# Pool branch of a hybrid decoder step as one stage: weights stationary, tokens moving

## The chip, the cores and the metric

One NeuronCore of a Trainium2 chip runs the whole program. The metric is the device time of one execution in microseconds.

## The reference

One layer for 1024 prompt tokens and 8 x 8 sample tokens, in float32. The part that matters here is the pool branch: the normed input times 512 columns of the input projection, causal means over 2, 4, 8 and 16 rows (one window for each group of 128 channels) minus the token itself, and a 128 x 128 mixing matrix per group.

```python
def pool_mix(ext, pos_base, w_pool):          # ext: history rows, then pool_in
    cs = cumsum(ext) with a zero row in front
    for gi, w in enumerate((2, 4, 8, 16)):
        c = slice(gi * 128, (gi + 1) * 128)
        means.append((hi[:, :, c] - lo[w][:, :, c]) / minimum(pos + 1, w))
    d = concatenate(means) - ext[:, 15:]
    return einsum('btgc,gcd->btgd', d, w_pool)
# layer: x += concat(rms_norm(attention), rms_norm(pool_mix)) @ w_out; then cross attention, MLP, final norm
# pool_in = rms_norm(x, g_norm1) @ w_in[:, 1304:1816]; also returned: the last 15 rows of pool_in
```

## The kernel before, in words

The kernel works in stages one after another: memory projection, input projection (q, k, v, gates), compression, sample attention, prompt attention, then the pool branch, the output projection (`mix_out`, L1539), cross attention and the MLP. Each stage writes its own program for each engine inside a Block, and allocates its buffers and semaphores in a `Phase` (L57). When a Phase ends, its semaphores are cleared and all engines meet at a barrier (L77 to L79), so a stage starts when the slowest engine of the one before is done. Inside a stage each engine runs its instructions in the order written, and semaphores alone tie the engines together.

Tokens lie in nine tiles: eight of 128 prompt tokens, one of the 64 sample tokens. The pool branch is two phases. The first is `project` (L94) with the tag `pin`: per tile, ScalarE sums the squares (L199) and takes the root (L202), VectorE scales x (L242), TensorE transposes the tile in eight blocks of 128 (L320), ScalarE writes the high part in fp32r (L210), VectorE the low part (L280). The weights are likewise split, eight slices of 128 rows, high part on ScalarE (L219), low part on VectorE (L291). Every product is made in three passes (high x high, high x low, low x high) with x stationary and 512 weight columns moving (L345): 24 matmuls per tile. VectorE copies the result, tokens on partitions, to `yp` (L302). The tiles come in the order 0, sample tile, 1 to 7. x has two slots; SP loads the first two tiles (L153), POOL the others, each when the tile two before it has been transposed (L184).

The second phase is `pool_mix` (L352): SP loads the history, the mixing weights and an edge table (L385 to L387), then the eight slices of w_out for the next stage (L389). TensorE waits for the first three, transposes `yp` and the history back to channels on partitions (L400), ScalarE copies them to `ext` (L417, L422). When all is written, VectorE makes the averages of group 0, 1, 2, 3 in turn by adding shifted copies (1, 2, 3, 4 adds, L440), an edge correction (L444) and the subtraction (L445, L448). TensorE mixes each group in plain float32, in pieces of 512, 512 and 64 columns (L408), and ScalarE copies the result to `mT` (L427).

`mix_out` begins with squares on ScalarE (L1644), and needs `aT`, `mT` and the w_out slices in `w_out_raw`, which lives through this stage and the pool branch.

Of the kernel before, what the change touches and what calls it, by code (L numbers as in the profile page):

```python
# [16 lines left out]
F32 = mybir.dt.float32  # L17
F32R = mybir.dt.float32r
I32 = mybir.dt.int32
ALU = mybir.AluOpType  # L20
# [32 lines left out]
def rows_of(i):  # L53
    return P if i < NT - 1 else DB * DT
# [294 lines left out]
    return n_stores[0]  # L349


def pool_mix(nc, t, ident, yp, mT, w_raw, s_w):  # L352

    seq_len = HIST + DT
    p_len = HIST + SEQ  # L360
    length = p_len + DB * seq_len
    with ExitStack() as ctx:
        ph = Phase(nc, ctx, "mix")
        ext = ph.sb("ext", [P, 4, length])
        sums = ph.sb("sums", [P, 2, length])
        diff = ph.sb("diff", [P, 4, TOK])
        state = ph.sb("state", [DB * HIST, PW])
        w = ph.sb("w", [P, 4, P])
        edge = ph.sb("edge", [P, 4, HIST])
        psT = [ph.ps(f"psT{k}", [P, 4, P]) for k in range(2)]  # L370
        psM = [ph.ps(f"psM{k}", [P, 512]) for k in range(2)]
        s_c = ph.sem("constants_loaded")
        s_tr = ph.sem("tile_transposed")
        s_ext = ph.sem("ext_written")
        s_d = ph.sem("difference_made")
        s_mm = ph.sem("mixed")
        s_m = ph.sem("mT_written")
        s_dve = ph.sem("vector_chain")
        samples = ext[:, :, p_len:length].rearrange("p g (b s) -> p g b s", b=DB)
        cols = [(0, 512), (512, 1024), (1024, TOK)]  # L380
        with nc.Block() as block:

            @block.sync
            def _(sp):
                sp.dma_start(state[:, :], t["state_pool"][0].rearrange("b s c -> (b s) c")).then_inc(s_c, 16)  # L385
                sp.dma_start(w[:, :, :], t["w_pool"][0].rearrange("g c d -> c g d")).then_inc(s_c, 16)
                sp.dma_start(edge[:, :, :], t["k_edge"]).then_inc(s_c, 16)  # L387
                for c in range(KC):
                    sp.dma_start(w_raw[:, c, :], t["w_out"][0][c * P:(c + 1) * P, :]).then_inc(s_w[c], 16)  # L389

            @block.tensor
            def _(pe):
                pe.wait_ge(s_c, 48)
                for k in range(NT + 1):
                    if k >= 2:
                        pe.wait_ge(s_ext, k - 1)
                    r = rows_of(k) if k < NT else DB * HIST
                    for g in range(4):
                        src = yp[0:r, k, g * P:(g + 1) * P] if k < NT else state[:, g * P:(g + 1) * P]
                        m = nc.tensor.transpose(psT[k % 2][:, g, 0:r], src, ident[0:r, 0:r])  # L400
                    m.then_inc(s_tr, 1)
                for g in range(4):
                    pe.wait_ge(s_d, g + 1)
                    for k, (a, b) in enumerate(cols):
                        u = 3 * g + k
                        if u >= 2:
                            pe.wait_ge(s_m, u - 1)
                        nc.tensor.matmul(psM[u % 2][:, 0:b - a], w[:, g, :], diff[:, g, a:b],  # L408
                                         start=True, stop=True).then_inc(s_mm, 1)

            @block.scalar
            def _(act):
                for k in range(NT + 1):
                    act.wait_ge(s_tr, k + 1)
                    if k < NT - 1:
                        dst, src = ext[:, :, HIST + k * P:HIST + (k + 1) * P], psT[k % 2][:, :, :]
                        nc.scalar.copy(dst, src).then_inc(s_ext, 1)  # L417
                        continue
                    n = DT if k == NT - 1 else HIST
                    for g in range(4):  # L420
                        dst = samples[:, g, :, HIST:seq_len] if k == NT - 1 else samples[:, g, :, 0:HIST]
                        m = nc.scalar.copy(dst, psT[k % 2][:, g, 0:DB * n].rearrange("p (b s) -> p b s", b=DB))  # L422
                    m.then_inc(s_ext, 1)
                for u in range(12):
                    g, (a, b) = u // 3, cols[u % 3]
                    act.wait_ge(s_mm, u + 1)
                    nc.scalar.copy(mT[:, g, a:b], psM[u % 2][:, 0:b - a]).then_inc(s_m, 1)  # L427

            @block.vector
            def _(dve):  # L430
                chain = Chain(dve, s_dve)
                chain(nc.vector.memset(ext[:, :, 0:HIST], 0.0))
                dve.wait_ge(s_ext, NT + 1)
                dve.wait_ge(s_c, 48)
                for g in range(4):
# [9 lines left out]
                    nc.vector.scalar_tensor_tensor(diff[:, g, 0:SEQ], cur[:, HIST:p_len], 1.0 / wide,  # L445
                                                   ext[:, g, HIST:p_len], ALU.mult, ALU.subtract)
                    tail = cur[:, p_len:length].rearrange("p (b s) -> p b s", b=DB)[:, :, HIST:seq_len]
                    nc.vector.scalar_tensor_tensor(diff[:, g, SEQ:TOK].rearrange("p (b s) -> p b s", b=DB), tail,  # L448
                                                   1.0 / wide, samples[:, g, :, HIST:seq_len], ALU.mult,
                                                   ALU.subtract).then_inc(s_d, 1)  # L450
                    dve.wait_ge(s_d, g + 1)


CMP_RAW = 3
# [1084 lines left out]
def mix_out(nc, t, x_of, aT, mT, x, raw, s_w, s_next):  # L1539

# [4 lines left out]
    with ExitStack() as ctx:  # L1545
# [1082 lines left out]
def build(nc, t, o):  # L2628

    with ExitStack() as ctx:  # L2630
# [9 lines left out]
        def x_of(i):  # L2640
            return x_p[i] if i < NT - 1 else x_s
# [75 lines left out]
        with ExitStack() as c2:  # L2717
            ph = Phase(nc, c2, "poolin")
            yp = ph.sb("yp", [P, NT, PW])
            sp_out = o["s_pool"][0]  # L2720

            def store_pool(eng, sem, i):
                if i == NT - 2:
                    eng.dma_start(o["p_pool"][0, 0], yp[P - HIST:P, i, :]).then_inc(sem, 16)
                    return 1
                if i == 0:
                    eng.dma_start(sp_out[:, 0:HIST - DT, :], t["state_pool"][0, :, DT:HIST, :]).then_inc(sem, 16)
                    return 1
                if i == NT - 1:
                    for b in range(DB):  # L2730
                        eng.dma_start(sp_out[b, HIST - DT:HIST, :], yp[b * DT:b * DT + DT, i, :]).then_inc(sem, 16)
                    return DB
                return 0

            project(nc, "pin", all_tiles, x_of, t["g_norm1"][0], t["w_in"][0][:, C_PI:C_END], PW, yp, store_pool, stored[1],
                    t, ident)
            pool_mix(nc, t, ident, yp, mT, w_out_raw, s_w_out)
        x = top.sb("x", [P, NT, DM])
        mix_out(nc, t, x_of, aT, mT, x, w_out_raw, s_w_out, s_cross_w)
        mix_scope.close()  # L2740
        up_raw, dn_raw = mlp_raw(w_out_raw)

# [23 lines left out]
```

## Time and profile before

| | us |
|---|---|
| median of three runs | 2049.45 (2046.32 to 2049.88) |
| the profiled execution | 2052.1, its span 2050.5 |
| TensorE busy, share of the span | 1813.2, 88% |
| VectorE busy | 1054.6, 51% |
| ScalarE busy | 839.3, 41% |
| DMA, mean over the span | 90 GB/s |

Engines are named PE (TensorE matmul), PEld (its weight load), DVE (VectorE), ACT (ScalarE), POOL and SP; an ending q marks an engine's queue. `a<-b` reads "writes a from b". In a timeline an idle time in brackets stands before the instruction, with what ended it. Ends of matmuls are modelled, so the spacing of their starts tells their pace. The mean granted clock of TensorE over the span is 0.926 of 2.4 GHz.

### The profile page before, as it was taken

How to read it: one execution, taken by the hardware profiler on the slowest of the kernel's cores; microseconds unless marked ns; L12 is line 12 of the kernel's file. 1: busy time of each engine (PE TensorE's matmuls, PEld its weight loads, DVE VectorE, ACT ScalarE, POOL GpSimd, SP SyncE). 2: the span in 40 equal slices, each digit the busy share in tenths (PEclk: the TensorE clock that was granted, in tenths of full speed). 3: DMA queues.
4: the chain of work that ended last, by engine and by line, in shares of the span. 5: the costliest groups of instructions: out<-in, count | busy, mean ns of one | idle time of the engine just before them, and what ended most of it. 6: DMA issues, size and time to landing. Idle time of an engine off the chain costs nothing. (4 is left out here: it accounts for less than half of the span.)

```text
span 2050.5 us, 26744 instructions
## 1 busy us (share of the span) xinstructions
PE 1813.2 (88%) x9784; PEld 1554.4 (76%) x9784; DVE 1054.6 (51%) x1927; ACT 839.3 (41%) x1698; POOL 199.3 (10%) x356
## 2 busy tenths in 40 slices
PE   5998667888888986869969997999999999999996
PEld 4897664676667775648747885999999999989996
DVE  3532565856778874364343434544446444454444
ACT  4320323446666664232145533433334433344443
POOL 0000402133333330010000000000000000000000
PEclk8998767968999998979979998999999999999998
DMA  4721405300000003240013111333334333353431
GB/s 173 232 90 44 124 10 156 94 9 1 1 1 1 1 1 103 88 168 38 1 62 109 57 42 40 138 123 132 123 123 155 124 123 123 123 177 142 162 125 66
DMA packets 111097, 184.56 MB, mean 90 GB/s; under 512 B 19248, under 2 KB 80112, under 8 KB 110919
## 3 DMA queue, kind: packets, MB, share of 16 engines
q1 hardware_dynamic: 100223, 159.29, 22.8%
q0 software_dynamic: 7408, 23.43, 3.3%
q8 instruction: 64, 1.05, 0.2%
q10 hardware_dynamic: 3360, 0.45, 0.2%
q14 instruction: 42, 0.34, 0.1%
HBM read 174.64 MB, written 12.73 MB: 91 GB/s over the span
## 5 line engine op out<-in xcount | busy, mean ns | idle before, releaser
L2511 DVE TENSOR_TENSOR mlp_dn_lo<-top_w_out_raw,mlp_dn_hi 128x1024 fp32r<-128x1024 f32 x96 | 117.6, 1225 | 299.5 <-ACT mlp_dn_hi L2434 299.5
L2351 PE MATMUL mlp_psU<-mlp_xT_hi,mlp_up_hi 128*128 128x384 f32 (+1 forms) x768 | 254.3, 331 | 5.3 <-DVE mlp_up_lo L2505 5.3
L2351 PE MATMUL mlp_psU<-mlp_xT_lo,mlp_up_hi 128*128 128x384 f32 (+1 forms) x768 | 252.5, 329 | 0.0
L2351 PE MATMUL mlp_psU<-mlp_xT_hi,mlp_up_lo 128*128 128x384 f32 (+1 forms) x768 | 252.4, 329 | 0.0
L2434 ACT CAST mlp_dn_hi<-top_w_out_raw 128x1024 fp32r<-128x1024 f32 x96 | 100.6, 1048 | 267.5 <-PE mlp_acc L2373 187.4
L2373 PE MATMUL mlp_acc<-mlp_dn_hi,mlp_h_hi 128*128 128x512 f32 x512 | 199.6, 390 | 0.0
L2373 PE MATMUL mlp_acc<-mlp_dn_lo,mlp_h_hi 128*128 128x512 f32 x512 | 199.4, 389 | 0.0
L2373 PE MATMUL mlp_acc<-mlp_dn_hi,mlp_h_lo 128*128 128x512 f32 x512 | 199.4, 389 | 0.0
L2351 PEld LDWEIGHTS mlp_psU<-mlp_xT_hi,mlp_up_hi 128*128 128x128 f32 x768 | 145.4, 189 | 9.4 <-issue 3.3
L2351 PEld LDWEIGHTS mlp_psU<-mlp_xT_lo,mlp_up_hi 128*128 128x128 f32 x768 | 145.4, 189 | 3.1
L2351 PEld LDWEIGHTS mlp_psU<-mlp_xT_hi,mlp_up_lo 128*128 128x128 f32 x768 | 145.3, 189 | 0.0
L1527 DVE TENSOR_TENSOR att_pT_lo<-att_psT,att_pT_hi 128x512 fp32r<-128x512 f32 (+1 forms) x148 | 102.0, 689 | 55.9 <-ACT att_pT_hi L1450 53.7
L2448 ACT ACTIVATE mlp_h_r<-mlp_psU 128x384 f32<-128x384 f32 (+1 forms) x96 | 45.5, 474 | 182.4 <-PE mlp_psU L2351 182.4
L2505 DVE TENSOR_TENSOR mlp_up_lo<-top_w_out_raw,mlp_up_hi 128x1024 fp32r<-128x1024 f32 x96 | 117.0, 1219 | 0.3 <-ACT mlp_up_hi L2428 0.3
L2373 PEld LDWEIGHTS mlp_acc<-mlp_dn_hi,mlp_h_lo 128*128 128x128 f32 x512 | 96.2, 188 | 20.1
L2373 PEld LDWEIGHTS mlp_acc<-mlp_dn_lo,mlp_h_hi 128*128 128x128 f32 x512 | 96.2, 188 | 16.3
L2373 PEld LDWEIGHTS mlp_acc<-mlp_dn_hi,mlp_h_hi 128*128 128x128 f32 x512 | 96.2, 188 | 16.3
L1450 ACT CAST att_pT_hi<-att_psT 128x512 fp32r<-128x512 f32 (+1 forms) x148 | 85.8, 590 | 51.3 <-PE att_psT L1394 51.2
L1394 PE MATMUL att_psT<-top_ident,att_prob 128*128 128x128 f32 (+1 forms) x592 | 98.5, 294 | 5.5 <-POOL att_prob L1308 2.5
L2428 ACT CAST mlp_up_hi<-top_w_out_raw 128x1024 fp32r<-128x1024 f32 x96 | 100.5, 1046 | 0.0
L2525 DVE TENSOR_TENSOR mlp_h<-mlp_h_r 128x384 f32<-128x384 f32 (+1 forms) x96 | 51.4, 536 | 86.6 <-ACT mlp_h_r L2448 86.6
L1394 PEld LDWEIGHTS att_psT<-top_ident,att_prob 128*128 128x128 f32 (+1 forms) x592 | 72.3, 147 | 15.2 <-issue 3.9
(408 smaller groups left out, 3996.2 us busy)
## 6 DMA issues: line engine op xcount, KB each, us to landing
top_w_out_raw<-in_w_up SPq DMA_DIRECT2D x48, 1024.0 KB
top_w_out_raw<-in_w_down SPq DMA_DIRECT2D x48, 1024.0 KB
cross_mem<-in_cache_mem_kv SPq DMA_DIRECT2D x8, 1024.0 KB, 4.8
qkv_w_raw<-in_w_in SPq DMA_DIRECT2D x8, 652.0 KB, 6.6
cmpin_raw<-in_cache_cmp_kv SPq DMA_DIRECT2D x36, 128.0 KB, 2.8
mem_w_raw<-in_w_mkv SPq DMA_DIRECT2D x8, 512.0 KB, 4.8
smp_sel<-in_cache_sel_kv SPq DMA_DIRECT2D x32, 128.0 KB
smp_sel<-in_cache_sel_kv POOLq DMA_DIRECT2D x32, 128.0 KB, 2.9
```

The source lines that it names most:

```text
L1394: m = nc.tensor.transpose(bank[kind, arg][0:w, hh, :], prob[:, HPG * (u % 2) + hh, c0:c0 + w], ident[:, :])
L1450: nc.scalar.copy(pT_hi[0:w, n % (LAG + 1), :], bank[kind, arg][0:w].rearrange("p a b -> p (a b)")).then_inc(s_th, 1)
L1527: nc.vector.tensor_tensor(pT_lo[0:w, n % (LAG + 1), :], bank[kind, arg][0:w].rearrange("p a b -> p (a b)"), pT_hi[0:w, n % (LAG + 1), :].b ...
L2351: m = nc.tensor.matmul(psU[n % 2][:, 0:w], a[:, u % 2, c, :], b[:, g % 2, c, 0:w], start=(c == 0 and n_pass == 0), stop=(c == KC - 1 and n ...
L2373: last = nc.tensor.matmul(acc[k][half][0:r, :], a[:, u % 2, at:at + r], b[:, u % 2, 512 * half:512 * half + 512], start=(first and n_pass ...
L2428: nc.scalar.copy(up_hi[:, u % 2], up_raw[:, k, :, a * P:(a + 1) * P]).then_inc(s_uh, 1)
L2434: nc.scalar.copy(dn_hi[:, u % 2], dn_raw[:, k, a, :]).then_inc(s_dh, 1)
L2448: nc.scalar.activation(h_r[:, 0:w], psU[n % 2][:, 0:w], ACT.Relu).then_inc(s_re, 1)
L2505: nc.vector.tensor_tensor(up_lo[:, u % 2], up_raw[:, k, :, a * P:(a + 1) * P], up_hi[:, u % 2].bitcast(F32), ALU.subtract).then_inc(s_ul, 1)
L2511: nc.vector.tensor_tensor(dn_lo[:, u % 2], dn_raw[:, k, a, :], dn_hi[:, u % 2].bitcast(F32), ALU.subtract).then_inc(s_dl, 1)
L2525: nc.vector.tensor_tensor(h_2[:, 0:w], h_r[:, 0:w], h_r[:, 0:w], ALU.mult).then_inc(s_h2, 1)
```

## The change

The two phases become one, `pool_branch`. The products are turned round: a 128 x 128 block of weights is stationary, xT moves. A unit is one channel group (128 channels) times one block of tokens: columns 0 to 256, 256 to 640, 640 to 1088. The result has channels on partitions, so the transposes of `yp` and `yp` itself go. xT (high and low) is kept whole. The x tiles lie in four slots in the upper half of `w_out_raw`; w_out slices are loaded when the slots come free. The tile order is 0 to 8, the sample tile last. The first block is made for all four groups together, slice by slice; the others unit by unit, groups in the order 3, 2, 1, 0. The averages and mixings of a group begin when its last unit is written. The last 15 prompt rows and the sample rows are transposed back from a small copy (`newest`) for the outputs. The wait for the pool output stores moves to the end of SP's program in `mix_out`.

```diff
-def pool_mix(nc, t, ident, yp, mT, w_raw, s_w):
+def pool_branch(nc, t, ident, x_of, mT, y_new, w_raw, s_w, s_pool, p_pool, s_st):
...
+        slots = work[:, 0:WS * PW].rearrange("p (k n) -> p k n", k=WS)
+        x_t = w_raw[:, KC - XS:KC, :]
+        blocks = [(0, 2 * P), (2 * P, 5 * P), (5 * P, TOK)]
+        groups = [3, 2, 1, 0]
+        units = [(g, 0) for g in groups] + [(3, 1), (2, 1), (3, 2), (2, 2), (1, 1), (1, 2), (0, 1), (0, 2)]
...
             def _(sp):
+                for i in range(2):
+                    sp.dma_start(x_t[:, i, :], x_of(i)).then_inc(s_x1[i], 16)
                 for c in range(KC):
+                    if c >= WS:
+                        sp.wait_ge(s_lo, c - WS + 1)
+                    sp.dma_start(slots[:, c % WS, :], t["w_in"][0][c * P:(c + 1) * P, C_PI:C_END]).then_inc(s_wi[c % WS], 16)
+                sp.dma_start(s_pool[:, 0:HIST - DT, :], t["state_pool"][0, :, DT:HIST, :]).then_inc(s_st, 16)
+                for c in (0, 1, 2, 3, 5, 6, 7, 4):
+                    sp.wait_ge(s_tr, 12 if c < KC - XS else 18 if c == KC - XS else 2 * (c + 1))
                     sp.dma_start(w_raw[:, c, :], t["w_out"][0][c * P:(c + 1) * P, :]).then_inc(s_w[c], 16)
+                sp.wait_ge(s_new, 1)
...
+            def _(pool):
+                for i in range(2, NT):
+                    if i >= XS:
+                        pool.wait_ge(s_tr, 2 * (i - XS + 1))
+                    pool.dma_start(x_t[0:rows_of(i), i % XS, :], x_of(i)).then_inc(s_x[i % XS], 16)
+                    if i == XS:
...
+                def product(u, c):
+                    g, k = units[u]
+                    a, b = blocks[k]
+                    for n_pass, (ws, xs) in enumerate(((w_hi, xT_hi), (w_hi, xT_lo), (w_lo, xT_hi))):
+                        m = nc.tensor.matmul(acc[u % 4][:, 0:b - a], ws[:, c, g * P:(g + 1) * P], xs[:, c, a:b],
+                                             start=(c == 0 and n_pass == 0), stop=(c == KC - 1 and n_pass == 2))
...
+                transposes(0)
+                transposes(1)
+                pe.wait_ge(s_tl, 4)
+                for c in range(KC):
+                    pe.wait_ge(s_lo, c + 1)
+                    for u in range(4):
+                        product(u, c)
+                    if c in (2, 4, 6):
+                        transposes(c // 2 + 1)
+                transposes(5)
+                unit(3, 1)
+                transposes(6)
+                unit(2, 1)
+                transposes(7)
+                transposes(8)
                 pe.wait_ge(s_c, 48)
+                pe.wait_ge(s_tl, 17)
...
+                unit(3, 2)
+                unit(2, 2)
+                unit(1, 1)
+                unit(1, 2)
+                mix(3)
+                unit(0, 1)
+                mix(2)
+                unit(0, 2)
+                pe.wait_ge(s_ext, len(units))
+                for g in range(4):
+                    m = nc.tensor.transpose(psT[1][0:HIST + DB * DT, g, :], newest[:, g, :], ident[:, :])
+                m.then_inc(s_nt, 1)
+                mix(1)
+                mix(0)
...
+                square_sum(0)
+                square_sum(1)
+                weight_hi(0)
+                hi(0)
+                weight_hi(1)
+                hi(1)
+                weight_hi(2)
+                weight_hi(3)
+                square_sum(2)
+                weight_hi(4)
+                hi(2)
+                weight_hi(5)
+                square_sum(3)
+                weight_hi(6)
+                hi(3)
+                weight_hi(7)
+                square_sum(4)
+                hi(4)
+                square_sum(5)
+                for g in groups:
+                    write(g, 0)
+                hi(5)
+                square_sum(6)
+                hi(6)
+                square_sum(7)
+                write(3, 1)
+                square_sum(8)
+                hi(7)
+                hi(8)
...
+                scale_x(7)
+                scale_x(8)
+                lo(7)
+                lo(8)
+                dve.wait_ge(s_hist, 1)
+                dve.wait_ge(s_c, 48)
+                dve.wait_ge(s_lo, KC)
+                for g in groups:
+                    averages(g)
...
+                sp.wait_ge(s_pool_stored, 16 * (DB + 2))
```

VectorE's program for the first tiles mirrors ScalarE's: `scale_x` for each `square_sum`, `lo` for each `hi`, `weight_lo` for each `weight_hi`. A unit's result is written by ScalarE (`write`): one copy for blocks 0 and 1, three for block 2 (prompt part, the rows for the outputs, sample part).

## Rows read from the trace of the kernel before

**Rows 1.** Windows: from:to, length, busy PE, PEld, DVE, ACT, POOL, clock, DMA share, GB/s.

```profile
783.10:796.80 13.70, 3.01 (x16) 2.50 (x17) 4.58 (x10) 6.87 (x13) 0.59 (x1) 0.53 0.56 154
796.80:859.50 62.70, 58.35 (x273) 46.18 (x272) 27.89 (x53) 20.21 (x43) 3.17 (x6) 0.97 0.22 76
859.50:900.90 41.40, 21.29 (x64) 11.63 (x64) 20.55 (x23) 10.87 (x29) 0.03 (x1) 0.71 0.31 115
900.90:914.00 13.10, 6.97 (x27) 6.04 (x28) 8.24 (x9) 9.16 (x11) 6.32 (x12) 0.61 0.79 295
```

**Rows 2.** Timeline, start of the branch: start us, duration us, engine, line, names, [idle before].

```profile
783.12 0.34 SPq L153 DMA_DIRECT2D pin_x_t<-in_x_prompt  x1
...
788.68 1.06 ACT L199 ACTIVATE pin_junk<-pin_x_t 128x1024 f32<-128x1024 f32 x1 [7.30 <-DMA pin_x_t<-in_x_prompt]
...
791.25 1.04 ACT L199 ACTIVATE pin_junk<-pin_x_t 64x1024 f32<-64x1024 f32 x1
...
792.39 1.97 PE L320 MATMUL pin_psT<-top_ident,pin_x_t 128*128 128x128 f32 x8 [11.78 <-DVE pin_x_t L242]
...
792.60 0.20 ACT L202 ACTIVATE pin_stat<-pin_stat 64x1 f32<-64x1 f32 x1 [0.21 <-DVE pin_stat L238]
```

**Rows 3.** Timeline of TensorE: starts of matmuls of 512, 256 and 384 columns.

```profile
858.12 0.39 PE L345 MATMUL pin_acc<-pin_w_lo,pin_xT_hi 128*128 128x512 f32 x1
...
858.35 0.39 PE L345 MATMUL pin_acc<-pin_w_hi,pin_xT_lo 128*128 128x512 f32 x1
...
1066.32 0.42 PE L1867 MATMUL cross_psS<-cross_kT_hi,cross_qT_hi 128*128 128x256 f32 x1
1066.53 0.41 PE L1867 MATMUL cross_psS<-cross_kT_lo,cross_qT_hi 128*128 128x256 f32 x1
...
1067.40 0.28 PE L1867 MATMUL cross_psS<-cross_kT_hi,cross_qT_hi 128*128 128x256 f32 x1
1067.52 0.28 PE L1867 MATMUL cross_psS<-cross_kT_lo,cross_qT_hi 128*128 128x256 f32 x1
...
1067.40 0.19 PEld L1867 LDWEIGHTS cross_psS<-cross_kT_lo,cross_qT_hi 128*128 128x128 f32 x1
...
1501.13 0.34 PE L2351 MATMUL mlp_psU<-mlp_xT_lo,mlp_up_hi 128*128 128x384 f32 x1
1501.30 0.34 PE L2351 MATMUL mlp_psU<-mlp_xT_hi,mlp_up_lo 128*128 128x384 f32 x1
```

**Rows 4.** Groups of instructions, 785 to 870 us: busy us, mean ns, idle before.

```profile
L280 DVE TENSOR_TENSOR pin_xT_lo<-pin_psT,pin_xT_hi 128x512 fp32r<-128x512 f32 x16 | 10.4, 687 | 3.5 <-ACT pin_xT_hi L210 3.5
...
L210 ACT CAST pin_xT_hi<-pin_psT 128x512 fp32r<-128x512 f32 x16 | 8.7, 589 | 25.6 <-PE pin_psT L320 25.6
L199 ACT ACTIVATE pin_junk<-pin_x_t 128x1024 f32<-128x1024 f32 x8 | 8.6, 1070 | 7.3 <-DMA pin_x_t<-in_x_prompt 7.3
...
L242 DVE TENSOR_SCALAR pin_x_t<-pin_x_t,pin_stat 128x1024 f32<-128x1024 f32 x8 | 6.0, 754 | 0.3
L291 DVE SCALAR_TENSOR_TENSOR pin_w_lo<-pin_w_raw,pin_gT,pin_w_hi 128x512 fp32r<-128x512 f32 x8 | 5.7, 749 | 5.0 <-ACT pin_w_hi L219 5.0
...
L219 ACT ACTIVATE pin_w_hi<-pin_w_raw,pin_gT 128x512 fp32r<-128x512 f32 x8 | 5.3, 716 | 5.3 <-DMA pin_w_raw<-in_w_in 5.3
```

**Rows 5.** Timeline, from the constants' transfer to the output stage.

```profile
866.32 1.57 PEld L400 LDWEIGHTS mix_psT<-top_ident,poolin_yp 128*128 128x128 f32 x8 [8.00 <-DMA mix_edge<-k_edge]
...
874.57 1.43 DVE L440 TENSOR_TENSOR mix_sums<-mix_ext 128x1222 f32<-128x1222 f32 x1 [12.27 <-ACT mix_ext L422]
...
888.18 1.43 DVE L440 TENSOR_TENSOR mix_sums<-mix_ext 128x1222 f32<-128x1222 f32 x1
...
888.20 2.23 PE L408 MATMUL mix_psM<-mix_diff,mix_w 128*128 128x512 f32 x6 [1.90 <-DVE mix_diff L448]
...
895.65 4.10 PE L408 MATMUL mix_psM<-mix_diff,mix_w 128*128 128x512 f32 x6 [5.21 <-DVE mix_diff L448]
...
900.88 0.63 ACT L1644 ACTIVATE out_sq<-mixed_aT 128x512 f32<-128x512 f32 x1 [0.71 <-PEq L79]
```

More of the change, by code:

```diff
@@ L361, in pool_mix @@
     length = p_len + DB * seq_len
+    n_old = DB * HIST
+    XS, WS = 4, 4
     with ExitStack() as ctx:
-        ph = Phase(nc, ctx, "mix")
+        ph = Phase(nc, ctx, "pool")
+        work = ph.sb("work", [P, 2 * length])
+        w_hi = ph.sb("w_hi", [P, KC, PW], F32R)
+        w_lo = ph.sb("w_lo", [P, KC, PW], F32R)
+        xT_hi = ph.sb("xT_hi", [P, KC, TOK], F32R)
+        xT_lo = ph.sb("xT_lo", [P, KC, TOK], F32R)
+        junk = ph.sb("junk", [P, DM])
+        gT = ph.sb("gT", [P, KC])
+        stat = ph.sb("stat", [P, 4, NT])
@@ new lines, in _ @@
+            @block.gpsimd
+            def _(pool):
[4 more added lines that the diff above has]
+                    if i == XS:
+                        pool.dma_start(state[:, :], t["state_pool"][0].rearrange("b s c -> (b s) c")).then_inc(s_c, 16)
+                        pool.dma_start(w[:, :, :], t["w_pool"][0].rearrange("g c d -> c g d")).then_inc(s_c, 16)
+                        pool.dma_start(edge[:, :, :], t["k_edge"]).then_inc(s_c, 16)
@@ L402, in _, with transposes @@
-                for g in range(4):
[L403 to L409, printed above, removed]
+                def transposes(i):
+                    r = rows_of(i)
+                    pe.wait_ge(s_xn, i + 1)
+                    for c in range(KC):
+                        if i and c % 4 == 0:
+                            pe.wait_ge(s_tl, 2 * (i - 1) + c // 4 + 1)
+                        m = nc.tensor.transpose(psT[c // 4][:, c % 4, 0:r], x_t[0:r, i % XS, c * P:(c + 1) * P],
+                                                ident[0:r, 0:r])
+                        if c % 4 == 3:
+                            m.then_inc(s_tr, 1)
@@ new lines, in unit, with mix @@
+                def unit(g, k):
+                    u = units.index((g, k))
+                    pe.wait_ge(s_ext, u - 3)
+                    pe.wait_ge(s_tl, 10 if k == 1 else 18)
+                    for c in range(KC):
+                        product(u, c)
+                def mix(g):
+                    pe.wait_ge(s_d, groups.index(g) + 1)
+                    for k, (a, b) in enumerate(cols):
+                        n = 3 * groups.index(g) + k
+                        if n >= 2:
+                            pe.wait_ge(s_m, n - 1)
+                        nc.tensor.matmul(psM[n % 2][:, 0:b - a], w[:, g, :], mT[:, g, a:b],
+                                         start=True, stop=True).then_inc(s_mix, 1)
@@ new lines, in hi, with weight_hi @@
+                def hi(i):
+                    r = rows_of(i)
+                    for h in range(2):
+                        act.wait_ge(s_tr, 2 * i + h + 1)
+                        nc.scalar.copy(xT_hi[:, 4 * h:4 * h + 4, i * P:i * P + r], psT[h][:, :, 0:r]).then_inc(s_th, 1)
+                def weight_hi(c):
+                    if c == 0:
+                        act.wait_ge(s_g, 16)
+                    act.wait_ge(s_wi[c % WS], 16 * (c // WS + 1))
+                    nc.scalar.mul(w_hi[:, c, :], slots[:, c % WS, :], gT[:, c:c + 1]).then_inc(s_hi, 1)
@@ L431, in _, with scale_x, lo, weight_lo @@
                 chain = Chain(dve, s_dve)
[L432 to L435, printed above, removed]
+                def scale_x(i):
+                    r = rows_of(i)
+                    dve.wait_ge(s_sum, i + 1)
+                    nc.vector.tensor_scalar(stat[0:r, 1, i:i + 1], stat[0:r, 0, i:i + 1], 1.0 / DM, EPS,
+                                            ALU.mult, ALU.add).then_inc(s_ms, 1)
+                    dve.wait_ge(s_sd, i + 1)
+                    chain(nc.vector.reciprocal(stat[0:r, 3, i:i + 1], stat[0:r, 2, i:i + 1]))
+                    nc.vector.tensor_scalar(x_t[0:r, i % XS, :], x_t[0:r, i % XS, :], stat[0:r, 3, i:i + 1], None,
+                                            ALU.mult).then_inc(s_xn, 1)
+                def lo(i):
+                    r = rows_of(i)
+                    for h in range(2):
+                        dve.wait_ge(s_th, 2 * i + h + 1)
+                        at = (slice(None), slice(4 * h, 4 * h + 4), slice(i * P, i * P + r))
+                        nc.vector.tensor_tensor(xT_lo[at], psT[h][:, :, 0:r], xT_hi[at].bitcast(F32),
+                                                ALU.subtract).then_inc(s_tl, 1)
+                def weight_lo(c):
+                    if c == 0:
+                        dve.wait_ge(s_g, 16)
+                    dve.wait_ge(s_hi, c + 1)
+                    nc.vector.scalar_tensor_tensor(w_lo[:, c, :], slots[:, c % WS, :], gT[:, c:c + 1],
+                                                   w_hi[:, c, :].bitcast(F32), ALU.mult, ALU.subtract).then_inc(s_lo, 1)
+                def averages(g):
+                    dve.wait_ge(s_ext, unit_no(g, 2))
                     wide = 2 << g
```

172 lines of the change are left out of this document (115 added, 57 removed).

## The prediction, made before the changed kernel was seen

> **What bounds it now.** I read the windows first, by stage: the pool branch runs from the first transfer at 783.12 to the first instruction of the output stage at 900.88, 117.8 us, in three pieces of different kind [rows 1, 2, 5]. Until 796.80 TensorE is nearly idle (busy 3.0 of 13.7 us) and waits for x and weights. From 796.80, its first product, to 858.74 it multiplies without a pause (58.35 of 62.7 us, clock 0.97): this piece is bound by TensorE. From 859.5 to 900.9 no engine is busy beyond 21.3 of 41.4 us, and the clock is 0.71: this is a chain. Its links stand in the timeline [rows 5]: TensorE idle 8.0 us behind the constants' DMA, transposes until VectorE starts at 874.57, then the four averages one behind the other until 895.6, and mixing at the half clock. This third piece is what the change can remove; what comes after 900.9 (output stage, cross attention, MLP) is untouched and starts when this branch ends, so whatever the branch gains, the end gains.
>
> **Part 1, until the first product.** Before: 13.7 us. x tile 0 lands 5.56 us after its issue, its squares, root and scaling take 3.7 us more, then come transposes at the half clock [rows 2]. New: tile 1 is a whole tile instead of the 64-row sample tile (256 KB more ahead of the weights), and POOL issues tiles 2 and 3 at once (1 MB) instead of behind the transposes. What a transfer costs under this load no row shows. Nearest rows: 154 GB/s ran in that window, 295 GB/s in the opening of the output stage, where both queues load [rows 1]. Lower bound 0 (tile 0 is issued first, and on another queue); upper bound: all 3 MB must land together, 3.1 MB at 295 GB/s is 10.5 us, so 5 us later than now. I take 1.0 us, near the lower bound, since tile 0 is still first. The Trainium skill, "DMA: Bandwidth & Descriptors", section "Issuing engines are not separate DMA queues", says that transfers of all issuing engines interleave on the same 16 DMA engines. That rule speaks against the early loads, and by it the cost would be nearer 5 than 1. Further: products now wait for both halves of tiles 0 and 1 (s_tl 4), and tile 1's transposes wait for tile 0's low halves. By hand from 789.7: root of tile 0 at 792.3, of tile 1 at 793.85 (1.55 us each on ScalarE, from 791.25 to 792.80 in [rows 2]), first weight slice 794.6, high parts of tile 0 until 796.0 (0.59 each [rows 4]), low parts 796.9 (VectorE makes a weight low part first, 0.75), transposes of tile 1 at the half clock 798.3, its high part 799.0, its low part 799.8. First product 799.9: **16.8 us instead of 13.7, +3.1**.
>
> **Part 2, until the last of unit (3,2).** Products: 12 units of 24, 288 instead of 216, but with 256, 384 or 448 columns. Spacing between starts at full clock: 512 columns 0.2265 us, 384 columns 0.173, 256 columns 0.12 [rows 3]; that is columns over 2.4 GHz plus 13 ns, so 448 give 0.20 (estimate). 96 x (0.12 + 0.173 + 0.20) = 47.3 us, against 216 x 0.2265 = 48.9. The weight load behind each is covered in all three. The Trainium skill, "TensorE: Matmul & The Clock Gate", section "The mechanism", states that a weight load overlaps matmuls in flight only if its row group differs; its section "LDWEIGHTS" prices 128 columns at 107 ns. By these two, 72 loads more would cost 7.7 us; the spacings of the rows contradict it, both at 256 columns and at 512.
> The order interleaves conversions with products, and here ScalarE, VectorE and TensorE wait for one another. ScalarE: 9 squares of 1.55, 16 high halves of 0.59 and two shorter ones, 8 weights of 0.72: about 30 us [rows 2, 4]. TensorE: block 0 11.5 us plus 2.2 us at the half clock (spacing 0.213 [rows 3] for the first two slices), transposes 1.1 per tile (half of the 1.97 at the half clock in [rows 2], rounded up), units (3,1), (2,1) 4.15 each, (3,2) 4.8: about 34. By hand, with a tile scaled 2.5 us after its square begins (1.55, then about 0.2 for the reciprocal and 0.75 [rows 4]), and ScalarE in its written order, which puts a tile's squares behind the previous tile's high parts: slices 0 to 2 end 806.5, tile 2 transposed 807.6, slices 3 and 4 810.5, tile 3 812.6 (1.0 us of waiting for its scaling), slices 5 and 6 815.5, tile 4 817.6 (1.0), slice 7 819.0, tile 5 821.9 (1.8), unit (3,1) 826.1, tile 6 827.2, unit (2,1) 831.4, tile 7 832.5, tile 8 834.5 (0.7, behind tile 7's low part), history 835.4, unit (3,2) **840.3: 40.4 us**. About 6 us of it is waiting; bounds: 34.4 (no wait) and 46 (twice the waits).
> Hidden, at zero: the constants on POOL's queue (needed at 835, issued behind tile 4 near 800; without cover they would cost some of the 8.0 us of now); the w_out slices, which SP issues as the x slots come free: the last waits for tile 8's transposes at 834.5, and the output stage needs it after 875; the old-history store, which sits on SP between. SP's wait for the new pool rows stands at its end, nothing is behind it but 9 stores of some 0.35 us.
>
> **Part 3, until the output stage.** Now from 840.3. VectorE's average of group 3 takes 7.4 us (888.18 to 895.6 [rows 5]); each group before it has one add less, and all four take 21.0 (from 874.57), so a step is 1.43 and groups 2, 1, 0 take 6.0, 4.5, 3.0. Group 3: written 841.3 (ScalarE's copies of 384, 79 and 64 columns, estimated at 1.0 us where one of 512 takes 0.59 [rows 4]), averaged 849.0, group 2 855.0, group 1 (unit (1,2) ends 854.1, written 855.1) 859.6. TensorE meanwhile: (2,2) 845.1, (1,1) 849.3, (1,2) 854.1, mix 3 856.3 (2.23 at full clock [rows 5]), (0,1) 860.5, mix 2 862.7, (0,2) 867.5. Tail: writing 1.0, newest rows transposed 0.6 (estimate, four transposes), mix 1 2.2 (869.1 to 871.4) beside the average of group 0 (868.6 to 871.6), mix 0 2.3, last copies 0.4, gap to the next stage 0.7: **875.0, so 34.7 us**. Bounds of the tail: +3.7 if the two last mixings run at the half clock (4.10 against 2.23 [rows 5]), nothing below. The averages, 21 us on the path now, leave it save 3 us of group 0, and even these lie beside mix 1.
>
> **Sum.** 16.8 + 40.4 + 34.7 = 91.9 against 117.8: 25.9 us less. Gone: 36 transposes of y with their copies, VectorE's copies into y, one phase seam, the wait for constants. Added: +3.1 at the start, 6 us of waits. The profiled execution took 2052.1 (span 2050.5), 2.65 above the median of the runs shown; on it the sum gives 2026.2, on the median 2049.45 - 25.9 = **2023.6**.
>
> **Rivals.**
> A: The front is bound by TensorE alone (my hand order too strict): part 2 takes 34.4 to 36, 5 us less: 2018.6. For it: ScalarE's 30 us fit beside 34. Against: the squares stand behind the high parts on an in-order engine. 0.12.
> B: Narrow products are bound by their weight loads, which last 0.19 [rows 3]: 96 x 0.07 + 96 x 0.017 = 8.4 us: 2032.0. Against it: in the same rows loads of that length stand beside starts 0.12 apart. 0.05.
> C: The early x loads share the DMA engines evenly, and tile 0 lands last: upper bound above, 5 - 1 = 4 us more, and weights late too: 2028 to 2031. For it: the engine share is already 0.56 in that window [rows 1]. 0.13.
> D, slower: the clock stays at half through parts 2 and 3, since waits stand between short units. After the first two slices 44 us of products would double, and 4 mixings add 1.9 each: 51 us, net +25: 2075. It decides from 26 us, half of that work at half clock. For it: 0.53 and 0.71 in the pieces with pauses [rows 1]; against: those had idle stretches of 11.8, 8 and 5 us [rows 2, 5], here none is over 2. 0.04.
> E: No gain within the bound, the branch spending 22 us elsewhere, as by D in part: 0.03.
> Forecast as summed: 0.63.
>
> **Numbers.** About 0.2% (4 us) is what a measurement of this kernel can tell from no change. Forecast with its bounds (part 1 -1/+4, part 2 -6/+6, tail +3.7) runs about 2017 to 2032; A, B and most of C are inside or at its edge. Range 2015 to 2034, leaving out D, E and the sum of all bad ends. Faster 0.93 (forecast, A, B, C), same 0.03 (E), slower 0.04 (D).
>
> **What would show it.** First product 16 to 18 us after the branch's first transfer; block 0's starts 0.12 apart; TensorE waits of 1 to 2 us before the transposes of tiles 3, 4 and 5, released by VectorE's scaling of x; group 3's average running beside units (2,2) and (1,1); branch of about 92 us; clock over 0.9 from 805 on. Wrong would be: spacing of 0.19 in block 0, tile 0 landing after 792, idle stretches of TensorE over 3 us in part 2, clock at half there, or a later output stage opening (a late w_out slice).

## The result, and the profile after

Four runs of the changed kernel had a median of 2017.36 us (2015.08 to 2025.71), against 2048.85 for the kernel before; the ratio is 0.9852, 95% interval 0.9833 to 0.9871, which is 26 to 34 us, about 1.5%, less. The forecast was 2023.6 in a range of 2015 to 2034. The profiled execution took 2019.2 us, its span 2017.2.

The branch itself went from 117.8 to 90.1 us (forecast: 91.9). It now runs from 780.67 to 870.74. Windows of its three parts in the changed kernel (from:to, length, busy PE, PEld, DVE, ACT, POOL, clock, DMA share, GB/s), which answer to [rows 1]:

```profile
780.60:795.10 14.50, 3.95 (x17) 3.18 (x17) 6.43 (x14) 8.38 (x15) 4.07 (x7) 0.54 0.86 298
795.10:836.10 41.00, 35.78 (x230) 33.83 (x231) 19.95 (x41) 21.41 (x51) 1.60 (x3) 0.91 0.49 174
836.10:870.70 34.60, 31.93 (x148) 25.57 (x146) 20.45 (x22) 9.54 (x27) 0.00 (x0) 1.00 0.02 5
```

TensorE now works through the last 34.6 us (31.9 busy, clock 1.00), where it was busy 21.3 of 41.4 at 0.71 before: the averages have gone beside the products. The middle has about as much work as forecast and 5.2 us without any. In the first part the DMA share is 0.86 instead of 0.56, at 298 GB/s instead of 154.

The start, which answers to [rows 2]:

```profile
780.67 0.82 SPq L420 DMA_DIRECT2D top_w_out_raw<-in_x_prompt  x2
...
784.32 1.06 ACT L533 ACTIVATE pool_junk<-top_w_out_raw 128x1024 f32<-128x1024 f32 x1 [5.39 <-DMA top_w_out_raw<-in_x_prompt]
...
789.25 0.72 ACT L548 ACTIVATE pool_w_hi<-pool_work,pool_gT 128x512 fp32r<-128x512 f32 x1 [0.55 <-DMA pool_work<-in_w_in]
...
791.28 0.72 ACT L548 ACTIVATE pool_w_hi<-pool_work,pool_gT 128x512 fp32r<-128x512 f32 x1 [0.35 <-DMA pool_work<-in_w_in]
...
795.06 0.58 PE L464 MATMUL pool_acc<-pool_xT_hi,pool_w_hi 128*128 128x256 f32 x1 [1.40 <-DVE pool_xT_lo L635]
```

Tile 0 begins its squares 3.65 us after its issue, where it took 5.56 before. The first two weight slices are waited for (0.55 and 0.35 us). The first product comes 14.4 us after the branch's start, 0.7 later than before, 2.4 earlier than forecast and ahead of the 16 to 18 us that the forecast named as its sign.

The spacing of products, which answers to [rows 3], is 0.12 us for 256 columns and 0.17 for 384; the weight loads beside them last 0.19:

```profile
799.26 0.28 PE L464 MATMUL pool_acc<-pool_xT_hi,pool_w_hi 128*128 128x256 f32 x1
799.26 0.19 PEld L464 LDWEIGHTS pool_acc<-pool_xT_lo,pool_w_hi 128*128 128x128 f32 x1
799.38 0.28 PE L464 MATMUL pool_acc<-pool_xT_lo,pool_w_hi 128*128 128x256 f32 x1
799.50 0.28 PE L464 MATMUL pool_acc<-pool_xT_hi,pool_w_lo 128*128 128x256 f32 x1
...
818.10 0.33 PE L464 MATMUL pool_acc<-pool_xT_hi,pool_w_hi 128*128 128x384 f32 x1
818.27 0.33 PE L464 MATMUL pool_acc<-pool_xT_lo,pool_w_hi 128*128 128x384 f32 x1
```

TensorE's waits in the front, from its timeline. Four stand where the forecast put them: 0.93 before the transposes of tiles 3 and 4 (the second at 810.78, not shown) and 1.75 before tile 5's, all three ended by VectorE's scaling of x (here named by the buffer the tiles lie in), and 1.06 before tile 8's. The fifth, 0.48 before the history's, was not forecast:

```profile
805.89 1.09 PE L455 MATMUL pool_psT<-top_ident,top_w_out_raw 128*128 128x128 f32 x8 [0.93 <-DVE top_w_out_raw L627]
...
815.06 1.09 PE L455 MATMUL pool_psT<-top_ident,top_w_out_raw 128*128 128x128 f32 x8 [1.75 <-DVE top_w_out_raw L627]
...
827.32 0.97 PE L455 MATMUL pool_psT<-top_ident,top_w_out_raw 64*128 64x64 f32 x8 [1.06 <-DVE pool_xT_lo L635]
828.76 0.50 PE L503 MATMUL pool_psT<-top_ident,pool_state 120*128 120x120 f32 x3 [0.48 <-DVE pool_xT_lo L635]
```

Behind the last two the clock falls, which was not forecast. Starts of the 448-column products of unit (3,2) are 0.37 us apart (448 columns at 1.2 GHz) until 832.7 and 0.2 after. The window from 829 to 832, which opens before the fall, has a mean clock of 0.57; from 829.5 to 832.5 it is 0.50:

```profile
829.70 0.57 PE L464 MATMUL pool_acc<-pool_xT_lo,pool_w_hi 128*128 128x448 f32 x1
830.07 0.58 PE L464 MATMUL pool_acc<-pool_xT_hi,pool_w_lo 128*128 128x448 f32 x1
...
832.96 0.37 PE L464 MATMUL pool_acc<-pool_xT_lo,pool_w_hi 128*128 128x448 f32 x1
833.16 0.37 PE L464 MATMUL pool_acc<-pool_xT_hi,pool_w_lo 128*128 128x448 f32 x1
```

```profile
829.00:832.00 3.00, 3.00 (x12) 2.57 (x11) 0.14 (x1) 0.82 (x5) 0.00 (x0) 0.57 0.58 187
```

The tail, which answers to [rows 5]: averages of group 3 from 836.91, mixing of group 3 inside the stream at 849.92, the last unit written and the average of group 0 begun at 864.03, mixing of group 0 at 867.13, output stage at 870.74:

```profile
836.91 1.43 DVE L651 TENSOR_TENSOR pool_work<-pool_ext 128x1222 f32<-128x1222 f32 x1 [7.76 <-ACT pool_ext L560]
...
849.92 1.45 PE L482 MATMUL pool_psM<-mixed_mT,pool_w 128*128 128x512 f32 x3
...
863.98 0.43 PEld L515 LDWEIGHTS pool_psT<-top_ident,pool_newest 128*79 128x79 f32 x4 [1.19 <-ACT pool_ext L560]
...
864.03 1.43 DVE L651 TENSOR_TENSOR pool_work<-pool_ext 128x1222 f32<-128x1222 f32 x1 [8.57 <-ACT pool_ext L560]
...
867.13 2.23 PE L482 MATMUL pool_psM<-mixed_mT,pool_w 128*128 128x512 f32 x6 [0.52 <-ACT mixed_mT L567]
...
870.74 0.63 ACT L1889 ACTIVATE out_sq<-mixed_aT 128x512 f32<-128x512 f32 x1 [0.90 <-PEq L79]
```

### The profile page after: what moved, and what is told of

The parts are those of the page before. It is cut to its first block and busy times, and to the rows that moved or that the text cites. A ratio compares the mean times of both kernels' runs of the same rounds, so it can differ in the third digit from the quotient of the medians.

```text
span 2017.2 us, 26797 instructions
## 1 busy us (share of the span) xinstructions
PE 1800.8 (89%) x9824; PEld 1554.3 (77%) x9824; DVE 1045.3 (52%) x1918; ACT 840.5 (42%) x1707; POOL 201.5 (10%) x359
```

## The experiments

All branch figures run from the issue of x tile 0 to the first squares of the output stage, in one profile each. Times are medians with the ratio to the kernel before, run in turn with it (2050.3 us with E1 to E4, 2050.0 with E5 to E7, 2050.6 with E8 and E9).

| kernel | time, us | ratio (95%) | until first product | branch | ahead of it | behind it |
|---|---|---|---|---|---|---|
| before | 2048.9 | 1 | 13.7 | 117.8 | 783.1 | 1149.6 |
| changed, first profile | 2017.4 | 0.9852 (0.9833 to 0.9871) | 14.4 | 90.1 | 780.7 | 1146.5 |
| E1 changed, again | 2020.3 | 0.9855 (0.9838 to 0.9872) | 14.45 | 89.7 | 781.6 | 1147.1 |
| E2 squares ahead | 2017.4 | 0.9834 (0.9817 to 0.9850) | 14.15 | 83.8 | 785.1 | 1149.2 |
| E3 averages last | 2037.5 | 0.9939 (0.9922 to 0.9956) | 14.6 | 103.8 | 782.4 | 1149.7 |
| E4 groups upwards | 2024.6 | 0.9882 (0.9862 to 0.9902) | 14.6 | 96.0 | 779.4 | 1147.1 |
| E5 late x | 2024.7 | 0.9883 (0.9868 to 0.9898) | 13.6 | 93.6 | 779.2 | 1149.3 |
| E6 seam only (kernel before) | 2043.8 | 0.9972 (0.9961 to 0.9983) | 13.2 | 112.6 | 780.6 | 1147.6 |
| E7 squares ahead, pause filled | 2014.7 | 0.9831 (0.9815 to 0.9846) | 14.6 | 83.0 | 780.5 | 1150.0 |
| E8 E7 with tiles 2 and 3 later | 2014.3 | 0.9821 (0.9800 to 0.9842) | 13.6 | 82.1 | 781.8 | 1147.3 |
| E9 changed, pause filled | 2019.2 | 0.9840 (0.9818 to 0.9862) | 14.4 | 87.0 | 782.8 | 1149.3 |

**E1.** The changed kernel, unedited.

> The changed kernel again, unedited. In the first profiled executions the pool branch took 117.8 us before and 90.1 us after (27.7 less), while the whole span shrank by 33.3. Theory 'the branch is all': the other 5.6 us (2.4 ahead of the branch, 3.1 behind it, in unchanged code) are scatter from one execution to another; here the branch takes 90 us again within 1, the parts outside it differ from the first profile by up to 3 us either way, and the ratio of the times corresponds to 26 to 30 us. Rival 'something outside the branch gained too': the part ahead of the branch again takes 780.7 and the part behind it 1146.5, each within 0.5 us, and the ratio corresponds to 32 us or more.

Measured: branch 89.7 us, ratio worth 29.7 us. The parts outside the branch, where no kernel here differs but for SP's wait for the pool stores at the end of `mix_out`, read 779 to 785 ahead of it and 1146.5 to 1150.0 behind it over all eleven profiles, with the kernel before and E6 inside that spread. So the 5.6 us of the first comparison outside the branch lie within what the profiles scatter, and the branch's length in the profile is the finer measure: it repeats within 0.4 us in the two profiles of the changed kernel. The times agree with it as far as they reach.

**E2.** ScalarE's order, and VectorE's with it:

```diff
                 weight_hi(4)
+                square_sum(3)
                 hi(2)
                 weight_hi(5)
-                square_sum(3)
                 weight_hi(6)
+                square_sum(4)
                 hi(3)
                 weight_hi(7)
-                square_sum(4)
+                square_sum(5)
                 hi(4)
-                square_sum(5)
                 for g in groups:
                     write(g, 0)
+                square_sum(6)
                 hi(5)
-                square_sum(6)
+                square_sum(7)
                 hi(6)
-                square_sum(7)
                 write(3, 1)
```

> ScalarE sums the squares of tiles 3 to 7 before the high parts of the tile in front (VectorE's scaling moves with it). Theory 'the front waits because the squares stand behind the high parts on an in-order engine': TensorE's waits of 0.9, 0.9 and 1.75 us ahead of the transposes of tiles 3, 4 and 5 vanish, those before tile 8 shrink, and the branch takes 85.5 to 87 us, 3.5 to 4.5 less than the changed kernel; the time falls by as much. Rival 'ScalarE is the bound of the front by its sum': waits only move to other places (high parts late instead of squares late) and the branch stays at 89 to 91 us.

TensorE's timeline of E2: tile 4's transposes without a wait, the pause before tile 8's as before, and unit (3,2) at full clock:

```profile
812.64 1.04 PE L455 MATMUL pool_psT<-top_ident,top_w_out_raw 128*128 128x128 f32 x8
...
827.12 0.96 PE L455 MATMUL pool_psT<-top_ident,top_w_out_raw 64*128 64x64 f32 x8 [1.06 <-DVE pool_xT_lo L635]
...
829.38 0.36 PE L464 MATMUL pool_acc<-pool_xT_lo,pool_w_hi 128*128 128x448 f32 x1
```

The three waits (3.6 us) are gone and the branch is 83.8 us, 5.9 shorter than E1, 1.4 more than the upper end expected. From the end of slice 2 to the start of unit (3,1) TensorE needs 10.6 us instead of 14.9, the three waits and 0.6 of restarting behind them; the first two units of block 2 take 9.8 us instead of 11.3 because the clock stays up. The time fell by about 4 us by the ratios (0.9855 and 0.9834, whose intervals overlap a little); in this profile the branch also started latest of all. The waits before tile 8 and the history did not shrink, as had been expected. The order was the cause of the three waits, and the rival that ScalarE's sum is the bound has fallen.

**E3.** The averages wait for all units; the mixings follow them:

```diff
-                    dve.wait_ge(s_ext, unit_no(g, 2))
+                    dve.wait_ge(s_ext, len(units))
...
                 unit(1, 2)
-                mix(3)
                 unit(0, 1)
-                mix(2)
                 unit(0, 2)
...
+                mix(3)
+                mix(2)
                 mix(1)
                 mix(0)
```

> The averages wait until all units are written, and all four mixings follow them; nothing else is undone. Theory 'the gain comes from running the averages beside the products': VectorE's 21 us lie on the path again, of which 3 did before, mixing of three groups leaves the stream of products (3.9 us earlier end of the last unit), the last mixing runs at the half clock (4.1 instead of 2.2 us): the branch takes about 105.5 us, 15.5 more than the changed kernel, and more than half of the 27.7 us are given back. Rival 'the gain is from the removed transposes of y, the seam and the wait for constants': at most 5 us more.

```profile
861.49 1.43 DVE L651 TENSOR_TENSOR pool_work<-pool_ext 128x1222 f32<-128x1222 f32 x1 [30.73 <-ACT pool_ext L560]
...
882.55 0.30 PEld L482 LDWEIGHTS pool_psM<-mixed_mT,pool_w 128*128 128x128 f32 x2 [0.97 <-DVE mixed_mT L659]
...
886.18 0.63 ACT L1889 ACTIVATE out_sq<-mixed_aT 128x512 f32<-128x512 f32 x1 [0.90 <-PEq L79]
```

VectorE's first average begins at 861.5, the last mixing at 882.55, the output stage at 886.2: branch 103.8, 14.1 more than E1. It is 1.4 less than expected; the last mixing stayed at the full clock (2.24 us, where 4.1 was expected). Half of the change's 28 us is this overlap, and the rival (5 us at most) has fallen. The time moved the same way: ratio 0.9939 against 0.9855, 17 us.

**E4.** The group order turned round (units, mixings and writes renamed alike):

```diff
-        groups = [3, 2, 1, 0]
+        groups = [0, 1, 2, 3]
```

> Groups in the order 0, 1, 2, 3, so that the long average (four adds, 7.4 us) comes last instead of the short one (one add, 3.05). Theory: what remains of VectorE on the path is the average of the last group alone, so the branch takes 4.35 us more (94.4 us), plus 1.9 if the last mixing falls to the half clock behind the longer pause. Rival 'TensorE's own work sets the tail': no more than 1 us, since mixing of group 2 runs beside the average.

The last mixing waits 5 us for the long average of group 3:

```profile
869.90 0.50 PEld L482 LDWEIGHTS pool_psM<-mixed_mT,pool_w 128*128 128x128 f32 x2 [5.02 <-DVE mixed_mT L659]
...
875.32 0.63 ACT L1889 ACTIVATE out_sq<-mixed_aT 128x512 f32<-128x512 f32 x1 [0.90 <-PEq L79]
```

Branch 96.0, 6.2 more than E1: 4.35 for the average, and 1.9 for the last mixing at the half clock, which took 4.1 us. Both terms are as expected; the rival has fallen. This part of the gain costs nothing but another order.

**E5.** POOL's loads as late as before:

```diff
-                    if i >= XS:
-                        pool.wait_ge(s_tr, 2 * (i - XS + 1))
+                    pool.wait_ge(s_tr, 2 * (i - 1))
```

> POOL loads x tiles 2 and 3 as late as the kernel before did (each when the tile two before it is transposed) and the later ones likewise; the four slots stay. In the changed kernel tile 0 began its squares 3.65 us after its issue, against 5.56 before, though 1 MB more was in flight. Theory 'the early loads cost tile 0 nothing': tile 0 still comes 3.4 to 3.9 us after its issue, the first product 14.2 to 14.6 us after it, and the branch stays at 89.7 within 1 us; in the front tile 2 may be short of time by up to 1 us. Rival 'they share the DMA engines to the branch's cost': tile 0 or the first weight slices land at least 1 us earlier, and the first product comes at 13.4 us or less. Second rival 'the early loads are what made part 1 quicker': the first product comes 1 us or more later.

```profile
779.20 0.82 SPq L420 DMA_DIRECT2D top_w_out_raw<-in_x_prompt  x2
...
782.79 1.06 ACT L532 ACTIVATE pool_junk<-top_w_out_raw 128x1024 f32<-128x1024 f32 x1 [5.34 <-DMA top_w_out_raw<-in_x_prompt]
...
792.78 0.29 PEld L463 LDWEIGHTS pool_acc<-pool_xT_hi,pool_w_hi 128*128 128x128 f32 x1 [1.80 <-DVE pool_xT_lo L634]
...
829.74 1.20 PE L454 MATMUL pool_psT<-top_ident,top_w_out_raw 64*128 64x64 f32 x8 [5.67 <-DVE pool_xT_lo L634]
```

The median time from issue to landing of the first four weight slices, in E1 and in E5:

```profile
pool_work<-in_w_in SPq DMA_DIRECT2D x4, 256.0 KB, 9.3
...
pool_work<-in_w_in SPq DMA_DIRECT2D x4, 256.0 KB, 6.0
```

The first theory was right on tile 0 alone, which came as early as in E1 (3.59 us after its issue), so sharing did not delay it. The first rival had the mechanism: the first four weight slices landed 3.3 us earlier, ScalarE no longer waited for two of them (0.49 and 0.36 us in E1), and the first product came at 13.6, 0.9 earlier than E1 and 0.2 short of what that rival asked for. So the early tiles share the engines to the slices' cost, not to tile 0's. The second rival has fallen. And with the loads late TensorE waited 5.7 us for tile 8, whose load starts behind the transposes of tile 6 instead of tile 4: the four slots are worth 4.6 us there, and the branch took 93.6, outside what the theory allowed.

**E6.** In the kernel before, the constants ahead and the stores' wait later (`constants_ahead`, not shown, issues the three loads behind the weight slices; the `...` inside the load of `w_raw` stands for the rest of the line):

```diff
-                sp.dma_start(state[:, :], t["state_pool"][0].rearrange("b s c -> (b s) c")).then_inc(s_c, 16)
-                sp.dma_start(w[:, :, :], t["w_pool"][0].rearrange("g c d -> c g d")).then_inc(s_c, 16)
-                sp.dma_start(edge[:, :, :], t["k_edge"]).then_inc(s_c, 16)
                 for c in range(KC):
                     sp.dma_start(w_raw[:, c, :], ...).then_inc(s_w[c], 16)
+                sp.wait_ge(s_stored, 16 * (DB + 2))
...
             project(nc, "pin", ...,
-                    t, ident)
+                    t, ident, wait_stores=False, ahead=constants_ahead)
```

> The kernel before with one part of the change: history, mixing weights and edge table are loaded by SP behind the weight slices of the projection, and its stores are waited for at the end of the second phase, not of the first. Products, transposes of y and the row of averages stay. TensorE's wait of 7.6 us before the first transpose of y shrinks to the gap between the phases, about 2 us: the branch takes 112 to 113 us instead of 117.8, and the time falls by 5 us. Theory 'overlap is most of the gain': what the changed kernel gains above this, 22 us, needs the averages beside the products. Rival 'the seam was most of it': 12 us or more here, since TensorE also stays at the full clock.

```profile
780.59 0.35 SPq L153 DMA_DIRECT2D pin_x_t<-in_x_prompt  x1
...
785.71 1.06 ACT L199 ACTIVATE pin_junk<-pin_x_t 128x1024 f32<-128x1024 f32 x1 [6.85 <-DMA pin_x_t<-in_x_prompt]
...
858.48 0.73 PE L394 MATMUL mix_psT<-top_ident,poolin_yp 128*128 128x128 f32 x5 [2.25 <-PEq L79]
```

The wait before the transposes of y is 2.25 us instead of 7.6, the branch 112.6 us, 5.2 less than before (0.4 of it ahead of the first product, where nothing was edited), and the time 3.5 to 8.0 us less by the interval (0.9961 to 0.9983 of 2050). A fifth of the change's gain could be had with these lines alone, and the rival (12 us or more) has fallen.

**E7.** On E2, unit (1,1) between the transposes of tiles 7 and 8 (ScalarE's writes of units (2,1) and (1,1) move ahead of the high parts of tiles 7 and 8, not shown):

```diff
                 unit(2, 1)
                 transposes(7)
+                unit(1, 1)
                 transposes(8)
...
                 unit(2, 2)
-                unit(1, 1)
                 unit(1, 2)
```

> The kernel with the squares ahead (83.8 us branch), and in it unit (1,1) moved between the transposes of tiles 7 and 8, where TensorE waited 1.1 and 0.5 us and, in two profiles of the changed kernel, ran the next 3.4 us at the half clock. Theory 'these waits and the clock behind them are on the path': the branch takes 81.5 to 83 us, and unit (3,2) runs at a spacing of 0.2 us from its first matmul on. The average of group 3 begins 3 us later, which costs nothing as long as its mixing, 8 us behind, finds it done. Rival 'the averages' chain takes the place of the wait': mixing of group 3 or 2 waits for VectorE by 1 us or more, and the branch stays at 83.8 or above.

```profile
827.30 0.60 PE L504 MATMUL pool_psT<-top_ident,pool_state 120*128 120x120 f32 x4 [0.76 <-DVE pool_xT_lo L635]
...
828.36 0.36 PE L464 MATMUL pool_acc<-pool_xT_hi,pool_w_hi 128*128 128x448 f32 x1
```

Branch 83.0, inside the expected range at its upper end: one wait of 0.76 remains, and the products of unit (3,2) stand 0.2 us apart. The averages did not become the bound. 0.8 us is less than the times can tell apart from E2.

**E8.** On E7, one wait on POOL ahead of its loads:

```diff
+                pool.wait_ge(s_x1[1], 16)
                 for i in range(2, NT):
```

> The kernel with squares ahead and the pause filled (83.0 us branch), and POOL waits for tile 1 to have landed before it loads tiles 2 and 3; later tiles as in the changed kernel. Late loads of all tiles had brought the first product from 14.45 to 13.6 us after the start of the branch, but tile 8 came 4.6 us late. Theory 'only tiles 2 and 3, in flight beside tile 0, 1 and the first slices, cost the front 0.9 us': first product at 13.4 to 13.8 us, no stall elsewhere, branch 82.0 to 82.4. Rival 'the cost moves': tiles 2 and 3 now ride beside slices 4 to 7, TensorE waits for a weight slice or for tile 2, and the branch stays at 83.

```profile
781.78 0.83 SPq L420 DMA_DIRECT2D top_w_out_raw<-in_x_prompt  x2
...
795.35 0.28 PEld L465 LDWEIGHTS pool_acc<-pool_xT_hi,pool_w_hi 128*128 128x128 f32 x1 [1.80 <-DVE pool_xT_lo L636]
```

First product 13.57 us after the start, branch 82.1, no wait of TensorE for a slice or for tile 2: as the first theory said. The first four slices landed in 6.1 us here too. With 0.9821 (0.9800 to 0.9842), some 37 us below the kernel before, this is the fastest kernel of the study by its median and by its branch; from E7 the times alone do not separate it.

**E9.** The edit of E7 on the changed kernel itself.

> The changed kernel with the pause filled (unit (1,1) between the transposes of tiles 7 and 8) but the squares in their old place. In all five profiles with the squares in the old place TensorE ran unit (3,2) at the half clock for about 3.5 us behind that pause; in the two with the squares ahead it did not, with the same pause in one of them. Theory 'this pause lets the clock fall, and whether it does depends on chance': unit (3,2) at full clock here, branch 1.1 + 0.3 + 1.6 = 3.0 us shorter than the changed kernel: 86.5 to 87. Rival 'the waits of the front before it (0.9, 0.9, 1.8 us) are the cause': the clock still falls somewhere behind tile 5's transposes, and the branch takes 88 to 89.

The window over the start of unit (3,2) has the clock at 1.00, where the changed kernel had 0.57 (829 to 832):

```profile
834.00:837.00 3.00, 3.00 (x18) 2.77 (x17) 0.00 (x0) 0.75 (x4) 0.00 (x0) 1.00 0.46 168
```

Branch 87.0, 2.7 less than E1. The waits of 0.9, 0.9 and 1.8 us did not by themselves let the clock fall. That the pause before tile 8 alone does it is not shown either: E2 had the same pause (1.06 us and 0.48) at full clock. It fell in all five profiles in which both stood (in E5 with 5.7 us in place of the 1.06), and in none of the four others: E2 lacked the three waits, E9 the pause, E7 and E8 both. No run tells this apart from chance further than that.

## Why the prediction was right

**What bounds it.** The reading of the kernel before held: the third piece was a chain, and E3 and E6 price it. Putting the averages back behind the products costs 14.1 us; the seam between the phases was worth 5.2. About 8.8 us of the 28.1 (117.8 less E1's 89.7) are left for what was not taken apart: the transposes of y, which held TensorE and VectorE's start from 866.3 to 874.6 [rows 5], the smaller total of columns, less the later start and the new waits. Since E3 and E6 edit different kernels, that remainder is an estimate. One reading was wrong: the kernel before did not multiply from 796.80 on without a pause. TensorE waited twice there, and the prediction's list of what goes leaves these 3.5 us out:

```profile
805.75 0.50 PE L345 MATMUL pin_acc<-pin_w_hi,pin_xT_hi 128*128 128x512 f32 x1 [2.26 <-DVE pin_w_lo L291]
...
808.61 1.07 PE L320 MATMUL pin_psT<-top_ident,pin_x_t 128*128 128x128 f32 x8 [1.21 <-issue]
```

**Part 1** (16.8 us forecast, 14.4 measured) was mis-sized, and the failed step is the 1.0 us added to tile 0's landing: it came 1.9 us earlier than in the kernel before, below the lower bound of 0 that the prediction gave. The hand-made chain from there to the first product (10.2) was near: 10.7, with 0.9 of waiting for weight slices. The contention is real, but E5 and E8 find it at the slices, and it costs 0.9 us. The Trainium skill, "DMA: Bandwidth & Descriptors", section "Issuing engines are not separate DMA queues", says that transfers interleave on the same 16 DMA engines whichever engine issued them. The traces agree: the first four slices, on SP's queue, took 9.3 us to land with 1 MB on POOL's queue and 6.0 without. The price that the forecast weighed, up to 5 us, did not come: 0.9 us, since tile 0, which everything waits for, landed in 3.6 us either way.

**Part 2** (40.4 forecast, 41.0 measured) was right in its waits: 1.0, 1.0, 1.8 and 0.7 were forecast before tiles 3, 4, 5 and 8, and 0.93, 0.93, 1.75 and 1.06 were measured. (These four add up to 4.5 us, not to the "about 6 us" on which the prediction's bounds rest; with the 0.48 before the history 5.2 were measured.) That the sum came so near is in part luck, since two errors cancel: everything until unit (3,2) was 1.3 us earlier relative to the first product than forecast, and that unit took 1.9 us longer, 1.5 of it at the half clock, which the sum had nowhere behind slice 1. Half clock in part 2 was one of the prediction's own signs of being wrong.

**The price of narrow products** stands: 0.12 and 0.173 us, so the 72 added matmuls cost no weight load, only the 13 ns that each spacing has beyond its columns (an estimate of 0.9 us in all). The 448-column spacing, estimated at 0.20, was 0.206 in this kernel. The rule of the Trainium skill, "TensorE: Matmul & The Clock Gate", section "The mechanism", that only another row group lets a weight load overlap, is contradicted by this trace as by the one before: loads of the full array, 0.19 us long, stand beside starts 0.12 us apart.

**Part 3** (34.7 forecast, 34.6 measured) was right step by step; E4 confirms that only the last group's average stands on the path.

**The rivals.** A (TensorE alone bounds the front) was wrong for the change as written, and E2 shows what its order withheld: 5.9 us. B and D fell with the spacing and the clock, E with the gain. C was right that the weights come late, at a fifth of its upper price, and wrong that tile 0 does.

**The rest of the miss.** The time came out 6.2 us below the forecast in the first runs and 3.3 in E1; 1.8 to 2.2 us of it are the branch. The rest, 4.4 and 1.1 us, lies outside it: 0.6 of the first is the median of the kernel before, which read 2048.85 in place of 2049.45, and the remainder is taken for scatter, as large as the 4 us that the forecast had named as its bound. No run shows a cause for it. Why tile 0 lands in 3.6 to 3.7 us in all profiles of the changed stage and in 5.1 to 5.6 in those of the old one (5.12 in E6), though more was in flight, stays open: this is the part of the near hit that was not understood; the second transfer in the queue is of 128 rows in the one and 64 in the other, and that was not tried by itself.

## What to carry to other kernels

When a stage is a chain (here no engine was busy for more than 21.3 of 41.4 us, at a clock of 0.71), cut the work so that its pieces finish at different times, and start the piece with the longest follow-up first: here the overlap gave 14 us and the order of four groups 6. On an in-order engine, write the step that another engine waits for ahead of the step that waits itself; a hand-made timetable from rows of the old trace found four of five such waits to 0.4 us before the kernel ran. And compare the length of the stage in the profile, not only the run times, when unchanged code scatters by more than the effect.

## What the runs showed of the hardware that was not expected

After waits of 0.93, 0.93, 1.75, 1.06 and 0.48 us, TensorE's granted clock went to 0.50 for about 3.4 us, and this cost 1.5 us (11.3 against 9.8 for two units, E1 and E2), though no single wait was over 1.8 us and the engine was busy 35.8 of 41.0 us. So it was in four profiles (the changed kernel, E1, E3, E4); without the first three waits (E2), or with the last two shortened to one of 0.76 (E9), it stayed at 1.00, in one profile each. In E5, where the pause before tile 8 was 5.7 us, the products behind it ran at the half clock as well. In E3 and E4 the last mixing behind waits of 0.8 and 5 us ran once at the full and once at the half clock (2.2 and 4.1 us).

A transfer of 512 KB issued first on SP's queue landed in 3.6 us with 2.5 MB issued behind it on two queues, while the first four 256 KB slices behind it took 9.3 us (median) with the 1 MB on POOL's queue (the changed kernel and E1), and 6.0 and 6.1 without it (E5 and E8). In the kernel before, where nothing was on POOL's queue at the start either, they took 6.5.
